# The first layer of the compressed attention branch: stationary and moving operands exchanged, four products side by side in column groups

## The reference, cut to what matters

```python
def compress(t, pos, w1, w2):
    seg = t.reshape(bsz, s // CMP_STRIDE, CMP_STRIDE, NSA_KV, NSA_DH)
    blocks = jnp.concatenate([seg[:, :-1], seg[:, 1:]], axis=2) + pos[None, None, :, None, :]
    flat = jnp.transpose(blocks, (0, 1, 3, 2, 4)).reshape(bsz, n_cmp, NSA_KV, CMP_LEN * NSA_DH)
    return jax.nn.gelu(flat @ w1) @ w2

kc = compress(k_c, cmp_pos[0], cmp_w1[0], cmp_w2[0])
vc = compress(v_c, cmp_pos[1], cmp_w1[1], cmp_w2[1])
```

## Time and profile before

| | us |
|---|---|
| median of 3 runs | 2424.62 |
| the runs | 2420.52, 2424.62, 2424.90 |
| the profiled execution | 2424.53 |
| its span, first to last instruction | 2422.8 |
| mean granted clock of TensorE in it | 0.991 of full |

### The profile page before, as it was taken

How to read it: one execution, slowest core, us unless ns; L and a number is a source line. 1 busy time by engine, 2 the same in 40 slices (tenths; PEclk the granted TensorE clock), 3 DMA queues, 4 the chain that set the end, 5 groups by cost and what they waited for, 6 DMA issues and landing times.

```text
span 2422.8 us, 40355 instructions
## 1 busy us (share of the span) xinstructions
PE 2384.5 (98%) x17632; PEld 2254.6 (93%) x17632; DVE 1391.2 (57%) x1724; ACT 1137.6 (47%) x1591; POOL 61.9 (3%) x110
## 2 busy tenths in 40 slices
PE   8999999999999999999999999999999999999998
PEld 6999999999999999999998999999999999999998
DVE  4446656554464465566444645586655645686665
ACT  5435436454354453454444444354545444355543
POOL 0000000000000000000000100000000100000000
PEclk9999999999999999999999999999999999999999
DMA  6564533455545545334655434344555433344553
GB/s 247 179 214 174 203 133 123 159 189 177 188 174 184 209 174 196 135 125 159 224 182 180 143 140 141 120 155 159 200 183 177 163 140 140 123 156 165 193 183 113
DMA packets 60255, 407.15 MB, mean 168 GB/s; under 512 B 7696, under 2 KB 9232, under 8 KB 12464
## 3 DMA queue, kind: packets, MB, share of 16 engines
q1 hardware_dynamic: 60080, 404.58, 46.7%
HBM read 401.93 MB, written 2.10 MB: 167 GB/s over the span
## 4 chain that ended last, share of the span: by engine, by line
PE 89%; DVE 4%; ACT 2%; DMA 2%; issue 1%; POOL 1%; SPq 0%; POOLq 0%; ACTq 0%; DVEq 0%
PE bank L394 27%; PE bank L396 27%; PE bank L395 27%; DVE w_lo L206 2%; DMA w_raw<-in_tiles 2%; DVE hT_lo L342 1%; PE bank L1844 1%; PE bank L1236 1%; PE bank L1631 1%; PE bank L1458 1%; PE bank L1847 1%; PE bank L1868 1%; PE bank L1318 1%; POOL x_rstd L276 1%; ACT w_hi L198 0%
## 5 line engine op out<-in xcount | busy, mean ns | idle before, releaser
L394 PE MATMUL bank<-hT_hi,w_hi 128*128 128x256 f32 x3408 | 974.3, 286 | 2.2 <-ACT b_dv L805 1.3
L395 PE MATMUL bank<-hT_lo,w_hi 128*128 128x256 f32 x3408 | 966.6, 284 | 0.0
L396 PE MATMUL bank<-hT_hi,w_lo 128*128 128x256 f32 x3408 | 966.6, 284 | 0.0
L206 DVE TENSOR_TENSOR w_lo<-w_raw,w_hi 128x2048 fp32r<-128x2048 f32 x370 | 843.0, 2285 | 129.9 <-ACT w_hi L198 129.6
L198 ACT ACTIVATE w_hi<-w_raw 128x2048 fp32r<-128x2048 f32 x370 | 705.3, 1909 | 190.0 <-DMA w_raw<-in_tiles 189.6
L394 PEld LDWEIGHTS bank<-hT_hi,w_hi 128*128 128x128 f32 x3408 | 655.3, 192 | 7.4 <-issue 1.9
L395 PEld LDWEIGHTS bank<-hT_lo,w_hi 128*128 128x128 f32 x3408 | 655.3, 192 | 2.6
L396 PEld LDWEIGHTS bank<-hT_hi,w_lo 128*128 128x128 f32 x3408 | 655.2, 192 | 0.0
L615 DVE TENSOR_TENSOR a_ffn_g<-a_ffn_act,bank 128x256 f32<-128x256 f32 x88 | 37.1, 421 | 339.7 <-ACT a_ffn_act L567 339.7
L394 PE MATMUL bank<-w_hi,hT_hi 128*128 128x256 f32 (+1 forms) x736 | 215.0, 292 | 12.3 <-DVE hT_lo L342 9.9
L396 PE MATMUL bank<-w_hi,hT_lo 128*128 128x256 f32 (+1 forms) x736 | 211.9, 288 | 0.0
(11 more groups left out here) (332 smaller groups left out, 2882.6 us busy)
## 6 DMA issues: line engine op xcount, KB each, us to landing
w_raw<-in_tiles SPq DMA_DIRECT2D x370, 1024.0 KB, 4.8
a_cmp_w<-in_cmp_w SPq DMA_DIRECT2D x2, 2048.0 KB, 8.1
a_gm_rows<-in_rows SPq DMA_DIRECT2D x2, 768.0 KB, 6.7
x_res<-in_x SPq DMA_DIRECT2D x2, 512.0 KB, 5.6
rel_line<-a_line SPq DMA_DIRECT2D x1, 1024.0 KB, 9.4
a_ret_rows<-in_rows SPq DMA_DIRECT2D x2, 512.0 KB, 8.1
b_rows<-in_rows SPq DMA_DIRECT2D x2, 512.0 KB, 6.7
out<-x_res SPq DMA_DIRECT2D x4, 256.0 KB, 2.0
```

The source lines that it names most:

```text
L206: dve.tensor_tensor(k.lo[slot][:], k.raw[slot][:], k.hi[slot][:].bitcast(F32), ALU.subtract).then_inc(k.lo_done[slot], 1)
L394: pe.matmul(out, w[0], x[0], start=start, stop=False)
L395: pe.matmul(out, w[0], x[1], start=False, stop=False)
L396: return pe.matmul(out, w[1], x[0], start=False, stop=stop)
```

## The change

Three things are done in each of the two layers of the first block:

- In each batch of 16 products the operands are exchanged. The windows (32 columns) are stationary, the chunk of `w1` (128 columns) moves, and product j writes to partitions 32(j mod 4) to 32(j mod 4) + 31 of bank 2 + i. So four partial sums, of four products each, stand one above the other in a bank, in the layout windows by hidden units.
- ACT copies the 128 x 128 bank to `parts[i]`, and after one more large product one matmul for each i, with `parts[i]` stationary and a 128 x 32 matrix `four` moving, adds the four partial sums and turns the result to hidden units by windows, into bank i, where it was before. `four` is four identity matrices one above the other.
- The two gelus of ACT come after both copies.

Once in the program, DVE makes `four` from the identity by a reduction, ahead of its first copy. The number of large products between the batch i = 1 and `cmp_kc` stays two.

```diff
@@ Compressed.scalar
         for i in range(2):
             f.scalar(act, f"cmp_hid{i}")
+            act.wait_ge(self.part_mm, i + 1)
+            act.activation(self.parts[i][:], self.k.bank[2 + i][:, 0:P], ACT.Copy).then_inc(self.part_ok, 1)
+        for i in range(2):
             act.wait_ge(self.hid_mm, i + 1)
             act.activation(self.hid[:, i, :, 0:16], self.k.bank[i][:, 0:32].rearrange("p (g n) -> p g n", g=2),
                            ACT.Gelu_apprx_tanh).then_inc(self.hid_ok, 1)
@@ Compressed.tensor
             for j in range(16):
-                last = pe.matmul(k.bank[i][:, 0:32], self.w1[:, i, j], self.win[i][:, j].rearrange("p g n -> p (g n)"),
-                                 start=(j == 0), stop=(j == 15))
-            last.then_inc(self.hid_mm, 1)
-        f.tensor(pe, 2)
+                q = slice(32 * (j % 4), 32 * (j % 4) + 32)
+                last = pe.matmul(k.bank[2 + i][q, 0:P], self.win[i][:, j].rearrange("p g n -> p (g n)"),
+                                 self.w1[:, i, j], start=(j < 4), stop=(j >= 12))
+            last.then_inc(self.part_mm, 1)
+        f.tensor(pe, 1)
+        pe.wait_ge(k.four_ok, 1)
+        for i in range(2):
+            pe.wait_ge(self.part_ok, i + 1)
+            pe.matmul(k.bank[i][:, 0:32], self.parts[i][:], k.four[:], start=True, stop=True).then_inc(self.hid_mm, 1)
+        f.tensor(pe, 1)
         f.mark("cmp_kc")
@@ Start.vector
         k, norm = self.k, self.norm
+        dve.wait_ge(self.small_in, 32)
+        dve.tensor_reduce(k.four[:], k.ident[:].rearrange("p (q n) -> p n q", q=4), AX.X, ALU.add).then_inc(
+            k.four_ok, 1)
         for h in range(DIFF_HEADS):
```

More of the change, by code:

```diff
@@ L140, in __init__ @@
         self.neg_half = sb("neg_half", [P, 32])
+        self.four, self.four_ok = sb("four", [P, 32]), ctx.enter_context(nc.semaphore("four_ok"))
         self.mean_sq, self.rstd = sb("x_mean_sq", [P, 2, NT, 2]), sb("x_rstd", [P, 2, NT])
@@ L1110, in __init__ @@
         self.hid, self.hid4 = r.at("cmp_hid", 20608, [P, 2, 2, N]), r.at("cmp_hid4", 21120, [P, 2, 4, N])
+        self.parts = [r.at(f"cmp_parts{i}", 26752 + 512 * i, [P, P]) for i in range(2)]
         self.kcT, self.vd = r.at("cmp_kcT", 22144, [P, N]), r.at("cmp_vd", 22272, [P, 2, 256])
@@ L1116, in __init__ @@
         self.pT = self.w1[:, 0, 0:4].rearrange("p a n -> p (a n)")
+        self.part_mm, self.part_ok = ph.sem("cmp_part_mm"), ph.sem("cmp_part_ok")
         (self.swap_in, self.small_in, self.w1_in, self.zeroed, self.win_ok, self.hid_mm, self.hid_ok, self.rep_ok,
```

## The result

The changed kernel takes 2411.14 us, the median of 5 runs (2407.45 to 2414.27), where the kernel before takes 2424.89 on the same chip; the ratio is 0.9941, 95% interval 0.9925 to 0.9956. A second measurement on another occasion gave 2410.74 (6 runs) and 0.9940 (0.9921 to 0.9958). So it is faster by 14 us. 10 us were forecast, and 2411.1 stands at the low edge of the range: by the ratio (0.9941 of the 2424.53 that the forecast started from is 2410.2) it is just outside. The direction and TensorE's own part of the sum were right; what is to be explained is a surplus of 4 us.

The account below looks back on a forecast made before the run. TensorE, busy 98% of the span, was taken to bound the kernel. Batches saving 9.52, less 0.90 for adding products, plus 1.5 of clock, made 10.1 us: 2424.53 to 2414.4, range 2411.0 to 2420.0, chance 0.45.

Parts of the forecast that it names:

- TensorE's own part: Four batches shortened from 3.57 to 1.19 us save 9.52 us; the new adding products cost 0.90 us.
- The batch: Each batch of 16 products: four column groups at once, 8 steps of 0.109 plus 0.32, 1.19 us instead of 3.57.
- B: Rival for the batches: half the overlap, a batch costs 2.10 us, kernel at 2418.0 us; chance 0.27.
- C: Rival for the batches: column groups follow one another, a batch costs 3.81 us, kernel at 2424.9 us; chance 0.13.
- D: Rival for the batches: weight loads not hidden under streaming, a batch costs 7.0 us, kernel at 2437.6 us; chance 0.05.
- The estimate by the 2.38 for three column tiles: Alternative batch cost, scaled to four tiles: 1.42 us a batch, whole sum 0.9 us less.
- The adding products: Two new products behind one large product in each layer: 0.45 us a layer, 0.90 added, without waiting.
- the start: DVE's reduction making `four`, done by 6.3 us, ahead of its first copy at 9.65: cost zero.
- E: Rival: TensorE waits at the new products for a late `w_hi` (1.90) in each layer, 2418.2 us; chance 0.10.
- The clock: Half-clock stretch of 3.42 us behind the second layer's first batch disappears: 1.5 us more saved.

Follow-up runs that it names:

- `four` last: The changed kernel with the buffer `four` allocated behind all others, so every other buffer lies as in the kernel before: 2415.25 us, ratio 0.9964.
- late pad: The kernel before plus 128 unused bytes per partition, allocated where the changed kernel has `four`, no instruction added: 2420.29 us, ratio 0.9985.
- between rows and weights: The kernel before plus an unused 128-byte buffer per partition between the transposed rows and the weight buffers: 2417.01 us, ratio 0.9965.

## Why the prediction was right and where it was wrong

- **The batch** was forecast at 1.19 and measured at 1.20; one, two and four groups take 32, 16 and 8 steps, so that B (2.10) and C (3.81) are out; four starts 0.007 apart also take away B's premise that records start no denser than each 0.055. The price of the entry and the exit, taken from another form of side by side, held to 0.02.
- **D**, loads that aren't hidden, did not happen: steps are 0.109 with four groups as with one. The rule of the Trainium skill ("TensorE: Matmul & The Clock Gate", The mechanism) that a load overlaps only where the row group differs does not hold for these groups, which share all rows. The estimate by the 2.38 for three column tiles that the Trainium skill gives ("TensorE: Matmul & The Clock Gate", Measured speedup vs the span model), 1.42 a batch, was too dear too: 32 steps became 8, and a batch cost 1.20.
- **The adding products and the start**: 0.45 each, no wait, no cost of the reduction itself. E (TensorE waits at the new products) did not happen; the tile had landed in time.
- **The sum of TensorE's own part**, 9.52 - 0.90 = 8.6, stood.
- **The start is the step that failed.** "Cost zero" was forecast: the instruction costs nothing, but its buffer moves all buffers behind it, and with them the distances of some 3,000 records: 3 us (even spans 2394.6 and 2391.4 to 2391.6 without and with the move). I did not look at addresses at all. With `four` last, the changed kernel takes 2415.25 us, near the forecast of 2414.4. That nearness is partly luck: its even span has 1.7 us that no term explains, against 2.9 of waits that the forecast left out.
- **The clock** was a term that was mis-sized: 1.5 us were forecast, and over the runs T is 8 to 12 us less than before, 4 to 5 us of time. The 1.5 was the one stretch of 3.42 us that the one profile had behind a batch; six profiles of kernels with narrow batches have 7.4 us on average there (3.3 us of time), at one batch or another, and the changed kernel's have none. The rest of the difference is not settled. With `four` last, T is 46.1 (standard error 2.6) against 47.6 (1.4) for before beside it, 0.7 us of time with an error of 1.3, though its profile too has nothing behind the batches; the kernel with the late pad has 44.4 against 47.6, the one between rows and weights 46.7 against 49.1.
- **What was not in the sum**: the 2 us given back at waits elsewhere. It was hidden behind the gain of the placement: the even span fell by 10.2 = 8.6 + 2.7 - 1.9, and 0.8 that is left over. With the 4 of the clock that is the 14 measured, where the forecast had 8.6 + 1.5.
- The range was too narrow by the placement and the clock. The clock could have been bounded better: the runs of the kernel before lie 4.4 us apart, and I let it take 3 beyond the forecast. The placement no row of before showed.

## What to carry to other kernels

Where a product needs few stationary columns, put the narrow operand there and run four products in column groups, each on another group than the one before it: n steps become n/4, for 0.2 us at the ends and one small product to add and turn. Where three products in a row stayed in one group, the same form gained nothing here. Try what stands around the stretches at the lower clock in other forms: here one product that streams 256 columns instead of 32, the rest for nothing, was worth 6 us. Before believing a small gain or loss, build the kernel with the addresses as they were: 128 unused bytes moved this kernel by 0 to 8 us, as to where they stood. And read a term of the clock from several profiles, not from one.

## What the runs showed of the hardware

- Four column groups that share all 128 rows run fully side by side, loads included, when consecutive products take different groups: four starts 0.007 us apart, then four more every 0.109 (8 steps for 32 records). With three products in a row on one group, 48 records took 4.65 us.
- Going into column groups costs 0.21 instead of 0.12 for the first step and 0.22 coming out, for one, two and four groups alike.
- The distance between records of a large product depends on where its two operands start in the partition: 229 to 230 ns against 233 to 235 with 512 columns, shorter where the two starts lie in different halves of 256 bytes. With 256 columns it is 118.6 against 120.0 in a part of the records only, and the rest of the rule is open. It predicted one kernel ahead (the pad between rows and weights), in direction, not in size.
- With 32 of 256 columns streamed in one large product T was 39.3 us, with all 256 it was 27.2, for the same even span. Stretches at the lower level stood in or behind products with 32 moving columns in every profile that has such products (the gates' in twelve, the batches' in six), though TensorE had no gap there, and in none once these streamed 128 or 256.
